# The triangular inverse of the recurrent stage kept in blocks of 32 for both heads, and grown together with its transpose

## The reference, cut to what matters

```python
# r, w, k, v, kk, a: (B, T, H, N); the state S is (B, H, N_value, N_key)
def frame_step(S, inp):
    r_t, w_t, k_t, v_t, kk_t, a_t = inp
    sa = jnp.einsum('bhvk,bhk->bhv', S, -kk_t)
    S = (S * w_t[:, :, None, :]
         + sa[..., None] * (kk_t * a_t)[:, :, None, :]
         + v_t[..., None] * k_t[:, :, None, :])
    o_t = jnp.einsum('bhvk,bhk->bhv', S, r_t)
    return S, o_t
```

## Time and profile before

| | us |
|---|---|
| median of 3 runs | 2098.58 (2097.71 to 2098.59) |
| span of the profiled execution | 2094.7 |
| PE busy | 2022.0 (97%) |
| DVE, ACT, POOL busy | 1032.5, 784.1, 909.8 |
| recurrent tiles j = 1 to 6, start to start | 72.5 to 73.9 each |

### The profile page before, as it was taken

One profiled execution on the slowest core, in us unless ns is written; L12 is line 12 of the kernel. 1 busy time (PEld: TensorE's weight loads), 2 busy tenths in 40 slices (PEclk: granted clock), 3 DMA queues, 4 the chain that ended last, 5 costly groups with the idle time before them and its releaser, 6 DMA issues.

```text
span 2094.7 us, 40435 instructions
## 1 busy us (share of the span) xinstructions
PE 2022.0 (97%) x16936; PEld 1598.3 (76%) x16936; DVE 1032.5 (49%) x1763; ACT 784.1 (37%) x1298; POOL 909.8 (43%) x724
## 2 busy tenths in 40 slices
PE   6999999999999999999999999999999999999997
PEld 5876667877888888877777777777787888888886
DVE  6343553243732231688778877876614366312212
ACT  4456664223432232444333333433234334322322
POOL 5334464444545454465233223323233455545442
PEclk9989999999999999999999999999999999999998
DMA  8520013422422222331111111111132322222221
GB/s 329 191 71 11 22 41 131 181 91 81 171 99 93 101 91 101 108 114 45 38 35 58 42 37 45 48 38 38 52 124 69 135 100 91 101 92 100 101 94 67
DMA packets 53059, 187.16 MB, mean 89 GB/s; under 512 B 6032, under 2 KB 7184, under 8 KB 52624
## 3 DMA queue, kind: packets, MB, share of 16 engines
q1 hardware_dynamic: 49104, 174.49, 23.5%
q10 hardware_dynamic: 3776, 10.09, 1.3%
HBM read 178.27 MB, written 6.29 MB: 88 GB/s over the span
## 4 chain that ended last, share of the span: by engine, by line
PE 89%; DVE 4%; ACT 2%; POOL 2%; issue 2%; DMA 0%; DVEq 0%; SPq 0%; ACTq 0%; POOLq 0%
PE psum L898 24%; PE psum L900 22%; PE psum L899 22%; PE psum L1360 2%; PE psum L1044 2%; PE psum L1065 1%; PE psum L1050 1%; PE psum L1352 1%; PE psum L1294 1%; POOL wlo L774 1%; PE psum L1326 1%; PE psum L1336 1%; PE psum L1304 1%; PE psum L1366 1%; PE psum L1083 1%
## 5 line engine op out<-in xcount | busy, mean ns | idle before, releaser
L774 POOL TENSOR_TENSOR wlo<-raw,whi 128x512 fp32r<-128x512 f32 x524 | 716.9, 1389 | 949.3 <-ACT whi L1485 949.3
L898 PE MATMUL psum<-ah,whi 128*128 128x512 f32 x1256 | 520.6, 415 | 3.8 <-DVE ah L1923 3.0
L899 PE MATMUL psum<-ah,whi 128*128 128x512 f32 x1256 | 495.8, 395 | 0.0
L900 PE MATMUL psum<-ah,wlo 128*128 128x512 f32 x1256 | 495.2, 394 | 0.0
L1485 ACT ACTIVATE whi<-raw 128x1024 fp32r<-128x1024 f32 x262 | 275.9, 1054 | 322.9 <-PE psum L900 318.0
L898 PEld LDWEIGHTS psum<-ah,whi 128*128 128x128 f32 x1256 | 238.9, 190 | 67.6 <-issue 11.3
L900 PEld LDWEIGHTS psum<-ah,wlo 128*128 128x128 f32 x1256 | 239.0, 190 | 52.6
L899 PEld LDWEIGHTS psum<-ah,whi 128*128 128x128 f32 x1256 | 239.5, 191 | 42.2 <-issue 0.2
L2244 DVE SCALAR_TENSOR_TENSOR x<-upad,vec,x 128x512 f32<-128x512 f32 x240 | 211.4, 881 | 5.8
L898 PE MATMUL psum<-hidden,whi 128*128 128x512 f32 x536 | 208.7, 389 | 0.0
L900 PE MATMUL psum<-hidden,wlo 128*128 128x512 f32 x536 | 208.5, 389 | 0.0
(11 more groups left out here) (378 smaller groups left out, 2874.1 us busy)
## 6 DMA issues: line engine op xcount, KB each, us to landing
raw<-in_w SPq DMA_DIRECT2D x300, 512.0 KB, 3.4
raw_first<-in_w SPq DMA_DIRECT2D x14, 512.0 KB, 9.5
raw_ck<-in_w SPq DMA_DIRECT2D x8, 512.0 KB, 7.3
x<-in_x SPq DMA_DIRECT2D x4, 512.0 KB, 6.1
x_kept<-x ACTq DMA_DIRECT2D x1, 2048.0 KB, 10.3
ao_kept<-ao ACTq DMA_DIRECT2D x8, 256.0 KB, 2.0
aof<-ao_kept ACTq DMA_DIRECT2D x1, 2048.0 KB, 10.6
x<-x_kept ACTq DMA_DIRECT2D x1, 2048.0 KB, 8.1
```

The source lines that it names most:

```text
L774: pool.tensor_tensor(lo_weight(place(s))[:, c], raw_of(SPLITS[s])[:, c], hi_weight(place(s)).bitcast(F32)[:, c], ALU.subtract).then_inc(lo ...
L898: pe.matmul(dst, wh, h_, start=first, stop=False)
L899: pe.matmul(dst, wh, l_, start=False, stop=False)
L900: return pe.matmul(dst, wl, h_, start=False, stop=last)
```

## The change

The inverse is kept as 32x32 blocks only, for both heads in one array: `ix`, `iy`, `ip` are 128 x (8 x 32) (`NB` = 8 is head and column tile, `BL` = 32). Four levels of growth remain. At each level `ip` is one group for both heads, with the level's masked copy `ml` (made beforehand by POOL) as the weights; then `ix` and `iy` come right behind one another, so that the inverse and its transpose grow by products, without a transpose at each level. The step from 32 to 64 is `jt` and `jy`: the block below the diagonal. `yf` holds the 64x64 result; POOL puts the diagonal blocks in.

`mb` of both heads becomes one entry `mbs` (the part for the inverse in 32-column pieces, then the part within the chunk, the heads in turn); `mk` becomes `mks`, with the heads in turn. ACT copies the unmasked part to `mc`, and DVE's read of the same bank waits for that. A tile has 13 slots where it had 16, `kk` stands one `part` later, and the taps are distributed anew. In the rows of the order below L1336 becomes L1361, L1352 becomes L1367, L1360 becomes L1374 and L1377.

```diff
-            + v[2:3] + [("lg2", j)] + v[3:] + ...
+    ... + v[:2] + [("mix", j, 0)]
+            + v[2:3] + [("kk", j), ("lg2", j)] + v[3:] + [("kkss", j), ("kkinv", j)] + g[:1] + ...
-TAPS = (0, 2, 3, 3, 2, 0, 2, 2, 4, 0, 2, 2, 0, 2, 0, 3)
+TAPS = (2, 0, 2, 3, 1, 1, 2, 3, 1, 3, 0, 3, 3)
-        out += [("conv", j, 2 if j else 0), ("tok", j, 0), ("mb", j, 0), ("tok", j, 1), ("mb", j, 1), ("iy0", j, 0), ("iy0", j, 1)]
+        out += [("conv", j, 3 if j else 0), ("tok", j, 0), ("mbs", j), ("iy0", j), ("tok", j, 1)]
...
-        out += [("tok", j, 2), ("tok", j, 3), ("mk", j, 0), ("mk", j, 1), ("inv", j, 0, 0)]
+        out += [("tok", j, 2), ("tok", j, 3), ("mks", j), ("inv", j)]
...
-        out += [("akv", j, 0), ("akv", j, 1), ("inv", j, 1, 0), ("opv", j)]
-        for lv in range(1, LEVELS + 1):
-            out += [("ip", j, 0, lv), ("ip", j, 1, lv)]
+        out += [("akv", j, 0), ("akv", j, 1), ("opv", j)] + slot()
+        for lv in range(1, LEVELS):
+            out.append(("ip", j, lv))
...
-            out += [("iy", j, 0, lv), ("iy", j, 1, lv)] + slot()
+            out += [("ix", j, lv), ("iy", j, lv)] + slot()
...
-            if lv < LEVELS:
-                out += [("inv", j, 0, lv), ("inv", j, 1, lv)] + slot()
+        out += [("yf", j), ("jt", j)] + slot() + [("jy", j)] + slot()
...
+                elif kind == "iy0":
+                    pool.wait_ge(mc_ready, 2 * j + 2)
+                    for lv in range(1, LEVELS):
+                        pool.tensor_tensor(ml[lv - 1], mc[:, :, 0:BL], level[lv].unsqueeze(1).to_broadcast([P, NB, BL]),
+                                           ALU.mult).then_inc(ml_ready, 1)
...
+                elif kind == "mbs":
+                    for t in range(TT):
+                        for q in range(4):
+                            n = (2 - q % 2) * BL
+                            for hh in range(2):
+                                mm = pe.matmul(b[BL * q:BL * q + BL, t * CH:t * CH + n], bh[rows, t * P + BL * q:t * P + BL * q + BL],
+                                               arow[rows, t, 0, BL * q:BL * q + n], start=True, stop=True)
...
+                elif kind == "ip":
+                    for n, q in own_blocks:
+                        mm = pe.matmul(b[q, n * BL:n * BL + BL], ml[lv - 1][q, n, :], ix[q, n, :], start=True, stop=True)
+                elif kind == "ix":
+                    for n, q in own_blocks:
+                        mm = pe.matmul(b[q, n * BL:n * BL + BL], iy[q, n, :], ip[q, n, :], start=True, stop=True)
+                elif kind == "iy":
+                    for n, q in own_blocks:
+                        mm = pe.matmul(b[q, n * BL:n * BL + BL], ip[q, n, :], iy[q, n, :], start=True, stop=True)
+                elif kind == "jt":
+                    for n, c in joined:
+                        mm = pe.matmul(b[down, n * BL:n * BL + BL], mc[up, n, BL:CH], ix[up, n, :], start=True, stop=True)
```

More of the change, by code:

```diff
@@ L46 @@
 LEVELS = 5
+BL = CH // 2
+NB = 2 * TT
 CONV = 31
@@ L224 @@
 RKV_SLOT = {1: 0, 0: 1, 2: 0}
-IN_BANKS = ("lw2", "la2", "lg2", "kkss", "bonus", "tok", "mb", "mk", "inv", "akv", "ip", "iy", "tav", "rr", "pt", "qq", "st", "gnm", "gnv", "kkb", "gnb")
+IN_BANKS = ("lw2", "la2", "lg2", "kkss", "bonus", "tok", "inv", "akv", "ip", "ix", "iy", "jt", "jy", "tav", "rr", "pt", "qq", "st", "gnm", "gnv", "kkb", "gnb")
 BLOCKS = weight_blocks()
@@ L344, in bank_order @@
             out += [("rb", "final"), ("rb", "mix2"), ("rb", "again")]
+        elif f[0] in ("mbs", "mks"):
+            out += [(f[0][:2], f[1], hh) for hh in range(2)]
         elif f[0] in IN_BANKS:
@@ L830, in _ @@
                 pool.memset(spare(i)[:, 0:1], 0.0).then_inc(zeros_done, 1)
-            psteps = 0
             for f in rwkv_order():
@@ L1286, in _ @@
                     b = bank(f)
-                elif kind not in ("opv", "opa", "ost"):
+                elif kind not in ("opv", "opa", "ost", "mbs", "mks"):
                     continue
@@ new lines, in _ @@
+                    for t in range(TT):
+                        for q in range(4):
+                            n = (2 - q % 2) * BL
+                            for hh in range(2):
+                                rows, b = slice(RN * hh, RN * hh + RN), bank(("mb", j, hh))
+                                mm = pe.matmul(b[BL * q:BL * q + BL, t * CH:t * CH + n], bh[rows, t * P + BL * q:t * P + BL * q + BL],
+                                               arow[rows, t, 0, BL * q:BL * q + n], start=True, stop=True)
@@ L1809, in _ @@
                         empty(f, (btok, ktok, vtk)[f[2] - 1][:, :, :], bank(f).rearrange("p (t n) -> p t n", t=TT))
-                elif kind == "inv":
-                    empty(f, ix[f[2]], bank(f)[:, 0:TT * CH].rearrange("p (t n) -> p t n", t=TT))
+                elif kind == "mbs":
+                    if j:
+                        wait_filled(act, ("jt", j - 1))
+                    for hh in range(2):
+                        wait_filled(act, ("mb", j, hh))
+                        act.activation(mc[:, TT * hh:TT * hh + TT, :], bank(("mb", j, hh))[:, 0:TT * CH].rearrange("p (t n) -> p t n", t=TT),
+                                       ACT.Copy).then_inc(mc_ready, 1)
+                elif kind in ("inv", "ix"):
+                    empty(f, ix, bank(f)[:, 0:NB * BL].rearrange("p (b n) -> p b n", b=NB))
                 elif kind == "akv":
@@ new lines, in _ @@
+                        dve.wait_ge(yf_ready, j)
+                    else:
+                        steps[0] += 1
+                        dve.tensor_copy(ti[:, :, BL:CH], own_eye.unsqueeze(1).to_broadcast([P, NB, BL])).then_inc(dve_step, 1)
+                    step(dve.tensor_tensor(ip, mc[:, :, 0:BL], level[0].unsqueeze(1).to_broadcast([P, NB, BL]), ALU.mult))
+                    dve.tensor_tensor(iy, ip, own_eye.unsqueeze(1).to_broadcast([P, NB, BL]), ALU.add).then_inc(iy0_done, 1)
+                elif kind in ("mbs", "mks"):
+                    for hh in range(2):
+                        name = (kind[:2], j, hh)
+                        wait_filled(dve, name)
+                        if j:
+                            dve.wait_ge(opa_done if kind == "mbs" else opv_done, j)
+                        if kind == "mbs":
+                            dve.wait_ge(mc_ready, 2 * j + hh + 1)
+                            within = bank(name)[:, TT * CH:].rearrange("p (t n) -> p t n", t=TT)
+                        else:
+                            full = bank(name).rearrange("p (t n) -> p t n", t=TT)
+                            within = full[:, :, CH:P]
+                            steps[0] += 1
+                            dve.tensor_tensor(ka[hh], full[:, :, 0:CH], strict.unsqueeze(1).to_broadcast([P, TT, CH]),
+                                              ALU.mult).then_inc(dve_step, 1)
+                        emptied_by(dve.tensor_tensor((mr if kind == "mbs" else kr)[hh].rearrange("p t (c n) -> p t c n", c=2),
+                                                     within.unsqueeze(2).to_broadcast([P, TT, 2, CH]),
+                                                     incl.rearrange("p (c n) -> p c n", c=2).unsqueeze(1).to_broadcast([P, TT, 2, CH]),
+                                                     ALU.mult), name)
```

159 lines of the change are left out of this document (74 added, 85 removed).

## The result

| | before | after |
|---|---|---|
| median, us | 2098.59 (2097.71 to 2099.53) | 2140.82 (2137.37 to 2145.28) |
| span of the profiled execution | 2094.7 | 2135.6 |
| PE busy | 2022.0 | 2014.7 |

The ratio is 1.0206, 95% interval 1.0194 to 1.0218. The forecast was 2097, with a range from 2083 to 2108. The change makes the kernel 42 us slower, and it does so although PE is busy for 7.3 us less.

A forecast was written before the change was run, and what follows sets the result against it. PE's own work was taken to bound the recurrent stage until another queue is late. Tiles 1 to 6 -1.0, tile 7 -3.1, tile 0 -1.9, together -6.0, clock +4.5: net -1.5 us, so 2097.1, range 2083 to 2108.

The forecast's parts named there:

- PE's saving in the inverse: PE's inverse for both heads: from 12.70 to 8.94 us, 3.76 us saved a tile.
- the sign to look for, PE busy near 67.5: Sign of the forecast: PE busy near 67.5 us in a tile, and the tile still near 72.
- The rival of a fixed 34 ns a record: Small products cost a fixed slot: the inverse takes 4.3 us more a tile, 2160 us in all; chance 0.01.
- The head: Start of a tile up to `gnv`: reached at +8.1 us, not 7.36; costs 0.7 us more, PE stands 1.7.
- The wait before glu's step: PE before the first step of the next tile's glu: waits 1.5 us (0.5 to 2.5) for its weights.
- the chain of `kk`: From `jt` through `kk` to POOL's low half of glu's weights: 13.9 us against PE's 12.8, a wait of 1.1.
- The first `st`: PE before a tile's first `st`: waits 1.9 us for `qs`, behind ACT's `whi`, 1.4 us more than before.
- Tile 0: First tile: has no `gnm`, gains 1.0 us in its head, -1.9 us together.
- The clock: Falls to half clock: four in seven heads at 1.3 us, some at the first `st`, +4.5 us.
- The rival "the clock decides": PE's pauses in head and before first `st` bring 14 falls, +17 us, +11 together: 2109 us; chance 0.23.
- The sum for a tile of 1 to 6: Each of tiles 1 to 6: -3.76 + 0.7 + 1.5 + 1.4 = -0.2 us, -1.0 together.

The follow-up runs named there:

- after_iy2: Changed kernel with each 32x32 product of `iy` issued twice, 256 more records a tile: 2204.8 us, 1.048 to 1.055 of the kernel before.
- after_head: Changed kernel with DVE's taps moved: one ahead of the head instead of three, none between last `st` and `upad`, four behind `pt`: 2125.6 us.
- after_yf0: after_yf with no tap ahead of the head and three behind `gnv` (before one and two): 2087.8 us.
- after_qs: Changed kernel with ACT's high and POOL's low half of the last glu's weights behind `qs` instead of ahead of it: 2122.7 us.
- before_pause: Kernel before, with ACT copying the first `qs` three times more before the copy that counts: 2116.5 us.
- after_yf: Changed kernel with `qs` ahead of the weights' high half, taps moved, single-step slots also between `ix` and `iy`, `kk` earlier, `yf` behind the last `iy`: 2086.4 us.
- after_dense: after_yf with `ix` and `iy` directly behind one another and four steps behind the pair: 2082.9 us.

## Why the prediction was wrong, step by step

- **PE's saving in the inverse: right but for one term.** A pair `ix`, `iy` was forecast at 1.28 us and takes 1.25. `jt` (0.63) fits; `jy` was put at 0.55 and takes 1.05 (row below; its output has 64 rows), so it goes by the bound from above. With these the inverse takes 9.4 us and not 8.9, 3.3 less than the 12.70 before. The whole tile's work fell by 3.6 us, where the sign to look for, PE busy near 67.5, meant 4.3. The rival of a fixed 34 ns a record is refuted as a law, but after_iy2 shows a price near it, 31 ns, where the supply binds.
- **The head: right.** `gnv` comes at +8.3 us in tile 4 (1268.38 - 1260.04) against 8.1 forecast, and PE stands 1.27 + 0.39 + 0.30 us against 1.7. DVE's taps make a part of it (after_head); the rest is not taps (after_yf0).
- **The wait before glu's step: mis-sized.** 0.86 us a tile instead of 1.5, and its cause is the bank that DVE's `mix` frees behind three taps, not the chain of `kk`. (The terms up to ACT's square add up to 4.45 and not 4.7; with them the chain would have given 0.85, the right number for the wrong reason.)
- **The first `st`: right**, 1.84 against 1.9, and after_qs confirms `whi` ahead of `qs`. The rows for the points so far:

```profile
1145.77 1.12 PE L1388 MATMUL psum<-iy,ti 32*64 32x32 f32 x32
...
1267.23 0.75 PE L1361 MATMUL psum<-eye_ones,iy 32*32 32x32 f32 x64 [1.27 <-DVE tmp L2495]
1268.38 1.05 PE L1468 MATMUL psum<-rw,sq 128*128 128x2 f32 x8 [0.39 <-ACT ktok L1559]
...
1314.31 0.47 PE L907 MATMUL psum<-ah,whi 128*128 128x512 f32 x1 [0.77 <-DVE rkv L2306]
```

- **Tile 0: wrong in sign.** It was to gain 1.9 us and lost 7.0: PE waits 2.12 us for `ix`, which ACT copies behind two of the norm's high halves, 1.2 for `rkv`, and 2.1 in gaps, and the tile is at half clock for 17 us instead of 10; I had looked at its head alone.
- **The clock: the term that was most mis-sized.** I counted four falls at 1.3 us in the heads and some at the first `st`, +4.5; it cost 21. The four in the heads came, and three at the first `st`, but three more stand at the gaps of the next point and one in tile 0, and a fall lasts 5.4 us on the mean, which costs some 2 us at 0.4 us for each us and not 1.3. The rival "the clock decides" had the mechanism: 14 falls and +17 for them, though its total of 2109 lacks the gaps. before_pause shows that a pause of 1.3 us a tile is enough, and after_qs and after_yf that taking a pause away gives back about 1.5 times its length and more.
- **Instruction supply: the step that was missing**, +20 us, and pauses of its own for the clock to fall behind. I priced small records at the 10.6 ns of the earlier trace rows, where 64 stand between two slots; there 140 records take 4.56 us (1110.95 to 1115.51), so 127 take some 4.1. In the changed kernel a level is 204 records in 5.1 us by my own terms, so 127 take 3.2, and the fetch needs 3.3 or more. The two "issue" gaps of the kernel before (0.9 us) were in its trace, and I read them as nothing; they too end 1.4 us after a packet.

The sum for a tile of 1 to 6, mean, was -3.6 of work, +3.5 of waits, +2.5 of gaps and some +2.6 of clock, 5.1 us more in all. In the same terms the forecast was -4.3 of work (67.5 against 71.75), +4.3 of waits (1.7, 1.5 and 1.9 against the 0.8 before), 0 of gaps and +0.7 of clock. The forecast took everything off the path that it could see on the other queues, and nothing for PE's own.

What stays open: what exactly starts a fall of the clock (equal pauses bring one in some tiles and none in others), and why a block's packet starts only 1.1 to 2.8 us after the resumption, and PE 1.2 to 1.6 us after it has landed.

## What to carry to other kernels

Count instructions as well as microseconds: where many small matmuls stand together, look for "issue" gaps inside groups, and whether they stand equally many records apart and each follows a packet of the instruction queue; then give each such stretch more large work, or keep the small products' number down. Before trusting an "issue" gap, look whether it is at the same place each time: then it is an ordinary wait whose releaser the profile did not find. A pause of PE costs more than its length, and PE work taken off pays only when the queues that feed it are moved as well: the same change lost 2% with its first order and gained 1.2% with another.

## What the hardware showed unexpectedly

- PE's instructions come in blocks of 256, which are some 127 float32 matmul records with their weight loads. Where PE has run out of them, it resumes 3.3 to 5.2 us after the resumption before, up to 6.1 with a weight load beside it, and each time 1.2 to 1.6 us after the block's packet has landed (268 gaps in 17 traces). Small records in surplus then cost 31 ns instead of 10.6 (after_iy2, gaps and clock together).
- A pause of 1.28 us instead of 0.57 before the first `st` of seven tiles and nothing else took the time at half clock from 24 to 55 us (before_pause).
- Of the same 128 small records, two groups with a slot between cost 0.2 to 0.3 us more than one pair (after_yf, after_dense).
